# Reordering the query tiles at the end of each attention pass: 7 6 5 4 3 1 0 2 in place of 7 to 0

## What is computed

```python
s = einsum('bqhd,bkhd->bhqk', q, k) * d ** -0.5
s = s + c[query] - c[key]                    # c: running sum of log forget gates
p = softmax(where(key <= query, s, -1e30))
out = einsum('bhqk,bkhd->bqhd', p, v)
```

## Time and profile before

| what | us |
|---|---|
| median of 3 runs (lowest, highest) | 2883.32 (2882.12, 2887.15) |
| the profiled execution's own time | 2876.48 |
| its span in the trace | 2874.7 |
| PE busy in the span | 2801.6 (97%) |
| DVE, ACT, POOL busy | 1706.5, 622.4, 1342.9 |

### The profile page before, as it was taken

How to read it: one execution, slowest core, us unless ns; L and a number is a source line. 1 busy time by engine, 2 the same in 40 slices (tenths; PEclk the granted TensorE clock), 3 DMA queues, 4 the chain that set the end, 5 groups by cost and what they waited for, 6 DMA issues and landing times.

```text
span 2874.7 us, 40988 instructions
## 1 busy us (share of the span) xinstructions
PE 2801.6 (97%) x14586; PEld 2068.4 (72%) x14586; DVE 1706.5 (59%) x4617; ACT 622.4 (22%) x1276; POOL 1342.9 (47%) x1140
## 2 busy tenths in 40 slices
PE   8999999999999999999999999999999999999998
PEld 4488888888876566564555777878878777777765
DVE  6655656656347777773777445677677772333226
ACT  2222221210025555551111101101111111111115
POOL 3533434547731110111454345677667665565545
PEclk9999999999999999999999999999999999999999
DMA  6500010111121113015434468899889989999986
GB/s 223 188 6 17 15 46 1 30 29 31 37 72 38 62 34 130 29 34 210 172 133 162 127 231 242 251 284 278 272 281 285 283 282 293 305 301 314 313 251 256
DMA packets 192573, 470.52 MB, mean 164 GB/s; under 512 B 27384, under 2 KB 108104, under 8 KB 166632
## 3 DMA queue, kind: packets, MB, share of 16 engines
q1 hardware_dynamic: 145424, 347.63, 33.9%
q0 software_dynamic: 44640, 111.84, 16.8%
q10 hardware_dynamic: 2304, 8.39, 0.7%
HBM read 349.64 MB, written 118.11 MB: 163 GB/s over the span
## 4 chain that ended last, share of the span: by engine, by line
PE 39%; DMA 8%; POOL 3%; DVE 2%; issue 1%; ACT 0%; POOLq 0%; SPq 0%; DVEq 0%; ACTq 0%
PE ps L3057 17%; PE ps L2832 8%; DMA base_rows<-moe_yo,index 5%; PE ps L3005 4%; DMA moe_xg<-t_rows,index 3%; PE ps L2976 3%; PE ps L2888 2%; PE ps L2973 2%; DVE moe_xT L2133 1%; PE ps L2898 1%; POOL moe_xg L2559 1%; POOL base_rows L2580 1%; PE ps L2851 1%; POOL moe_fin L2641 1%; PE ps L2842 0%
## 5 line engine op out<-in xcount | busy, mean ns | idle before, releaser
L2559 POOL DMA_INDIRECT moe_xg<-t_rows,index x433 | 422.8, 976 | 166.5 <-issue 118.8
L3057 PEld LDWEIGHTS ps<-moe_xT,moe_wg 128*128 128x128 f32 x2048 | 353.6, 197 | 53.6 <-issue 29.6
L3057 PE MATMUL ps<-moe_xT,moe_wg 128*128 128x192 f32 (+22 forms) x2048 | 380.2, 339 | 8.7 <-DVE moe_hh L2033 8.6
L3057 PE MATMUL ps<-moe_xT,moe_wu 128*128 128x192 f32 (+22 forms) x2048 | 375.3, 336 | 0.0
L2133 DVE STREAM_TRANSPOSE moe_xT<-moe_xg 128x256 f32<-128x256 f32 x433 | 235.1, 609 | 209.6 <-DMA moe_xg<-t_rows,index 203.9
L2580 POOL DMA_INDIRECT base_rows<-moe_yo,index x100 | 228.9, 2289 | 279.2 <-DVE moe_yo L2147 98.8
L3057 PEld LDWEIGHTS ps<-moe_xT,moe_wu 128*128 128x128 f32 x2048 | 353.3, 196 | 4.3
L1342 POOL TENSOR_TENSOR fox_diag<-fox_c,fox_causal 128x128 f32<-128x128 f32 x128 | 55.8, 457 | 425.0 <-DVE fox_mx L1371 420.1
L2696 ACT ACTIVATE moe_sl<-ps 128x256 f32<-128x256 f32 (+19 forms) x144 | 49.8, 346 | 928.0 <-PE ps L3057 833.1
L1365 DVE CUSTOM_DVE_ANT_0 hT<-ps,fox_c 128x512 f32<-128x512 f32 (+7 forms) x320 | 166.6, 560 | 81.7 <-PE ps L1627 81.4
L2188 DVE SCALAR_TENSOR_TENSOR moe_yo<-ps,weight,moe_yo 128x512 f32<-128x512 f32 (+14 forms) x280 | 187.4, 741 | 27.7 <-ACT moe_yo L2719 27.7
(11 more groups left out here) (376 smaller groups left out, 5020.7 us busy)
## 6 DMA issues: line engine op xcount, KB each, us to landing
moe_wg<-in_we_gate SPq DMA_DIRECT2D x64, 1024.0 KB
moe_wu<-in_we_up SPq DMA_DIRECT2D x64, 1024.0 KB
moe_wd<-in_we_down SPq DMA_DIRECT2D x64, 1024.0 KB, 9.7
fox_c<-ck SPq DMA_DIRECT2D x8, 1032.0 KB, 8.8
emb_xin<-in_x SPq DMA_DIRECT2D x16, 512.0 KB, 4.3
h_rows<-emb_hr SPq DMA_DIRECT2D x16, 512.0 KB, 2.8
ret_w<-in_w_in SPq DMA_DIRECT2D x16, 512.0 KB, 6.5
moe_yt<-h_rows SPq DMA_DIRECT2D x16, 512.0 KB, 5.5
```

The lines of the kernel that those rows point to most:

```text
L2559: pool.indirect_dma_start(out=xg[g % NXG][:, :], out_offset=None, in_=quarters, in_offset=bass.IndirectOffsetOnAxis(ap=route.index4[:, AT4 ...
L3057: ins = pe.matmul(out, w[:, c, f:FF:FC], xT[u][:, c, 0:n], start=(c == 0), stop=(c == DC - 1))
```

## The change

Every pass takes its tiles in the order 7 6 5 4 3 1 0 2. Tile 0 has a single round. The scores list hands out four units in round 1.0 (tile 2's) and three in round 2.2 (the last of tile 7). Tile 0's `inverse` comes on DVE in the last round of tile 1, its `keep` ahead of the next tile's copies on ACT, and in round 0.0 DVE takes the `bias` of the two units due before the copies, while PE turns tile 2 after the scores in place of before them.

```diff
-        order = [(p, t) for p in range(PAIRS) for t in range(TILES - 1, -1, -1)]
+        order = [(p, t) for p in range(PAIRS) for t in (7, 6, 5, 4, 3, 1, 0, 2)]
...
-        ROUNDS = [3 if t == 0 and n + 1 < NT else len(groups[n]) for n, (_, t) in enumerate(order)]
+        ROUNDS = [len(x) for x in groups]
...
-            scores_in[n, i] = [later.pop(0) for _ in range(2) if later and later[0][0] <= most]
+            scores_in[n, i] = [later.pop(0) for _ in range(3 if order[n][1] == 2 and i == 2 else 4 if order[n][1] == 1 and i == 0 else 2) if later and later[0][0] <= most]
...
@@ DVE
+                    if i == ROUNDS[n] - 1 == 0:
+                        for m, u in scores_in[n, i]:
+                            bias(m, u)
                     if i == ROUNDS[n] - 1 and n + 1 < NT:
                         for s in groups[n + 1][0]:
                             back(n + 1, s)
-                    if i == (2 if HALF[n] else 0):
+                        if len(groups[n + 1]) == 1:
+                            inverse(n + 1)
+                    if i == (2 if HALF[n] else 0) and len(groups[n]) > 1:
                         inverse(n)
                     if i == len(groups[n]) - 1 and i >= 1:
                         finish(n)
-                    for m, u in scores_in[n, i]:
+                    for m, u in (scores_in[n, i] if ROUNDS[n] > 1 else []):
                         bias(m, u)
                     if len(groups[n]) == 1 and i == 0:
                         finish(n)
@@ ACT
+                    if len(groups[n]) == 1 and i == 0:
+                        keep(n)
                     if i == ROUNDS[n] - 1 and n + 1 < NT:
                         for s in groups[n + 1][0]:
                             back(n + 1, s)
                     for m, q, a in exps_last.get((n, i), ()):
                         exps(m, q, a)
-                    if i == spread_at[n]:
+                    if len(groups[n]) > 1 and i == spread_at[n]:
                         keep(n)
@@ PE
-                    if i == ROUNDS[n] - 1 and n + 1 < NT:
+                    if i == ROUNDS[n] - 1 >= 1 and n + 1 < NT:
                         for s in groups[n + 1][0]:
                             turn(n + 1, s)
...
                     for m, u in scores_in[n, i]:
                         scores(m, u)
+                    if i == ROUNDS[n] - 1 == 0 and n + 1 < NT:
+                        for s in groups[n + 1][0]:
+                            turn(n + 1, s)
```

## The result

The changed kernel is slower: 2894.70 us in the median of seven runs (2892.39 to 2897.65) against 2885.53 for the kernel before on the same chips (2882.12 to 2887.70), a ratio of 1.0031 with a 95% interval of 1.0021 to 1.0040. That is some 9 us more. The forecast was 2895.7, which is 12.4 more than the 2883.3 that it started from.

The account below looks back on a forecast made before the run. PE, busy 97% of the span, was taken as the bound. New waits of 6.8 against 3.3 us saved, over three ends 10.5, plus 1.9 in the last pass: 12.4 on 2883.3 gives 2895.7 us, range 2885.5 to 2902.

Parts of the forecast that it names:

- (e): Tile 7's units 6 to 8 in a row at a pass's end: unit 8 waits for unit 6's bias, 0.45 us lost.
- (a): Tile 2's four units in a row with two bank pairs: unit 2 waits for banks, 0.9 us lost.
- (b): Tile 0's first product waits for tile 1's `finish` behind the reduction and tile 0's `inverse` on DVE: about 1.05 us lost.
- (c): Tile 2's first product waits for tile 0's `finish`, behind tile 7's first bias and a copy on DVE: 0.75 us lost.
- (d): Tile 7's first transposes wait for its exponentials: a chain of 8.3 us against PE's cover of 6.24, 2.05 lost; the largest.
- (f): Second half of tile 7: chain 8.3 us against PE's cover of 7.4, 0.9 to 1.0 lost in place of 0.51.
- (g): Tile 6's units begin in round 7.0 in every pass: its wait becomes 1.64 us in place of 1.07, 0.57 more.
- the 3.3 that went: Saved at each end of passes one to three: waits of 1.97 (tile 0's scatter), 0.76 (banks), 0.51 us (tile 7's second half).
- one such fall before and one after: PE's clock falls at one pass's end in both kernels, 1.7 us lost each time, so no difference.
- the fall of the clock at every end: Rival: (d)'s wait drops PE's clock at all three ends, 2 times 1.7 us more, 2899.1 us; chance 0.13.
- The wash: Rival: DVE and ACT keep up, (a) to (c) vanish, 0.8 us an end remains, last pass level, about 2886; chance 0.16.
- The faster case: Rival: old waits and first clock fall go, nothing comes; tile 2's work hides tile 7's exponentials; 10.9 us, 2872.4; chance 0.09.

## Why the prediction was right

Sign and places came out, and the size roughly: 12.4 was forecast, 8.5 measured in the attention and 9.2 between the medians. That the median of 2894.70 lies within 1 us of 2895.7 is luck in part, since the kernel before came out at 2885.53 over seven runs, 2.2 above the start of the forecast. The walk through the queues is confirmed step by step, except that no run takes (e) away. Idle time at the second end, forecast and measured: (a) 0.9 and 0.86; (b) 1.05 and 0.81; (c) 0.75 and 0.74; (d) 2.05 and 1.91; (e) 0.45 and 0.56; (f) 0.9 to 1.0 and 0.69; (g) 0.57 more, and 0.57 (1.64 for 1.07). Together 6.1 for 6.8, against the 3.3 that went; an end became 2.77 us longer (119.47 to 122.24), 3.5 was forecast. The last pass lost 1.6 for 1.9: its (b) was 0.58, not 1.05, and tile 2's exponentials cost 0.93, not 0.6.

The terms mis-sized: (b), (d) and (f) were 0.24, 0.14 and 0.31 too high, as PE's cover was longer than walked, 6.42, 6.40 and 7.84 in place of 6.15, 6.24 and 7.4: in (b) units 2 and 3 take 1.69 (1063.07 to 1064.76) and not 1.5, in (d) eight products, taken by proportion as 0.83, last 0.91. The chain of (d) itself is 8.31 (1075.45 to 1083.76), as walked. With (e) and the idle time that went this makes 2.2 us over three ends. In (b) the walk has the whole wait behind DVE's queue; 0.58 of it is the chain that the earlier trace rows showed and stays when the queue is short. And "one such fall before and one after" failed: the clock did not fall in the changed kernel's attention, so the first end lost 1.3 (120.65 to 121.97) and not 2.8. The prediction's terms for the last pass add up to 1.8, not to 1.9, and the waits that it puts at "some 15 us" to 16.8. The ends, the clock and the last pass make the 3.9 us between the forecast 12.4 and the 8.5 measured in the attention.

The rivals: the fall of the clock at every end did not come, with three waits of 1.9 us, each ahead of transposes, at 1.00. The wash fell with (a) to (c) at 0.86, 0.81 and 0.74, and its mechanism, DVE's order, turned out to be the smaller part of (b). The faster case fell at (d): the chain of 8.31 us did not fit into its cover of 6.40.

## What to carry to other kernels

When a wait at a seam is to be filled with other work, first look whether the late instruction can be moved alone: here a few lines on an engine with idle time won 9 us by the timed ratio, and the reordering around them lost that and as much again. When work is moved in front of a consumer, count how much of the producer's chain still has cover: in the old order tile 7's scores were started early enough to hide its exponentials. Units that go into two pairs of banks in turn gain nothing from being issued four in a row: the third waited 0.86 us.

## What was not expected of the hardware

The four scalings behind `inverse` took 1.11 us at three ends and 0.87 in the last pass, and that is the difference of the two values of (b), 0.81 and 0.58. Timeline of DVE and GpSimd in the changed kernel:

```profile
1066.32 0.88 POOL L1342 TENSOR_TENSOR fox_diag<-fox_c,fox_causal 128x128 f32<-128x128 f32 x2 [1.45 <-DVE fox_mx L1371]
1066.56 1.11 DVE L1406 TENSOR_SCALAR fox_rd<-ident,fox_rinv 128x128 f32<-128x128 f32 x4
...
1310.54 0.87 DVE L1406 TENSOR_SCALAR fox_rd<-ident,fox_rinv 128x128 f32<-128x128 f32 x4
```

At the three ends GpSimd makes the next pass's masks at that moment; in the last pass there are none to make. The Trainium skill, page SBUF — State Buffer, section on who interferes with whom, says that VectorE and GpSimd share a pair of ports that one instruction holds alone while the other waits, and names this kind of VectorE instruction among those that can take it. The trace agrees: 0.24 us at a time here, and only VectorE was held up (GpSimd's two took 0.86 to 0.89 with the scalings beside them and without). The masks as the cause are shown by the other runs, which move the scalings: in all ten traces the four take 1.10 to 1.19 us where a mask is being made beside them, and 0.87 or 0.88 everywhere else. With tile 0's reciprocals behind `finish`, or early in the old order (1069.12 above), they meet no mask and take 0.87.

A wait of 1.97 us in front of a scatter was followed by a fall of the clock at one end of three, 1.9 us at none of three, and 2.03 us ahead of tile 2's transposes in the last pass in one execution of two. Two of the ten traces have a fall in the first tile 7, behind a wait of 1.21 us that all ten have. A fall is worth 1.2 to 1.5 us here, and from these runs it can't be told in advance which wait brings it.
